# The 128-row block of the wide experts as three fp32r products, and the order of the first two experts

## The reference

```python
def moe_swiglu(h, router_w, w_gate, w_up, w_down):
    logits = xf @ router_w                      # 256 tokens, 8 experts
    top_val, top_idx = lax.top_k(logits, 2)
    gates = jax.nn.softmax(top_val, axis=-1)
    ...
    # for each expert, over the tokens that chose it (1024 -> 2816 -> 1024):
    y = (jax.nn.silu(x @ w_gate[e]) * (x @ w_up[e])) @ w_down[e]
    # out[token] += gate * y
```

## Time and profile before

| | |
|---|---|
| median of 3 runs | 1466.91 us (1465.32 to 1468.29) |
| the profiled execution, its own time | 1468.1 us |
| its span, first to last instruction | 1466.3 us |
| TensorE busy in the span | 96% |
| VectorE busy, ScalarE busy | 34%, 28% |
| bytes read from HBM | 383.77 MB |

### The profile page before, as it was taken

One profiled execution on the slowest core, in us unless ns is written; L12 is line 12 of the kernel. 1 busy time (PEld: TensorE's weight loads), 2 busy tenths in 40 slices (PEclk: granted clock), 3 DMA queues, 4 the chain that ended last, 5 costly groups with the idle time before them and its releaser, 6 DMA issues.

```text
span 1466.3 us, 23253 instructions
## 1 busy us (share of the span) xinstructions
PE 1414.9 (96%) x10140; PEld 1021.0 (70%) x10140; DVE 505.3 (34%) x747; ACT 407.2 (28%) x707; POOL 107.5 (7%) x133
## 2 busy tenths in 40 slices
PE   7999999999999999998999999999998999999996
PEld 7979988888888979988555645555544455555553
DVE  5667546666665657545100010101010100011112
ACT  5467436434345467444100000000000000000001
POOL 6200000000006000000100000101010100010100
PEclk9999999999999999998999999999999999999998
DMA  9308533555552217526746679999999996489995
GB/s 362 112 3 324 190 116 115 186 187 192 194 200 91 84 72 287 188 101 258 288 176 276 274 293 421 421 420 420 421 421 421 421 421 270 175 342 373 421 421 207
DMA packets 55138, 387.32 MB, mean 264 GB/s; under 512 B 6368, under 2 KB 6752, under 8 KB 9216
## 3 DMA queue, kind: packets, MB, share of 16 engines
q1 hardware_dynamic: 54112, 384.07, 66.1%
q10 hardware_dynamic: 432, 1.08, 0.2%
q0 software_dynamic: 496, 0.74, 0.2%
HBM read 383.77 MB, written 2.10 MB: 263 GB/s over the span
## 4 chain that ended last, share of the span: by engine, by line
PE 85%; DMA 6%; DVE 4%; ACT 3%; issue 1%; SPq 0%; DVEq 0%; ACTq 0%
PE banks L1845 40%; PE banks L1601 9%; PE banks L1603 9%; PE banks L1602 9%; PE banks L1774 6%; DMA raw_of_parts<-in_pieces_dram 4%; PE banks L1776 3%; DMA raw<-in_pieces_dram 2%; PE banks L1824 2%; PE banks L1809 2%; PE banks L1895 1%; PE banks L1721 1%; PE banks L1749 1%; PE banks L1625 1%; ACT w_high L827 1%
## 5 line engine op out<-in xcount | busy, mean ns | idle before, releaser
L1180 DVE TENSOR_TENSOR w_low<-raw,w_high 128x2048 fp32r<-128x2048 f32 x93 | 214.8, 2311 | 134.0 <-ACT w_high L827 133.9
L827 ACT ACTIVATE w_high<-raw 128x2048 fp32r<-128x2048 f32 x93 | 178.0, 1915 | 68.5 <-PE banks L1776 65.5
L1845 PE MATMUL banks<-raw,token_rows 128*64 128x256 f32 (+3 forms) x1480 | 161.3, 352 | 3.1 <-DMA raw<-in_pieces_dram 3.0
L1845 PE MATMUL banks<-raw_of_parts,token_rows 128*32 128x128 f32 (+4 forms) x1448 | 154.7, 344 | 2.8 <-DMA raw_of_parts<-in_pieces_dram 2.8
L1845 PEld LDWEIGHTS banks<-raw,token_rows 128*64 128x64 f32 (+2 forms) x1480 | 93.8, 132 | 71.6 <-issue 48.0
L1601 PE MATMUL banks<-rows,w_high 128*128 128x256 f32 x480 | 137.4, 286 | 2.0 <-DVE rows L1181 2.0
L1845 PEld LDWEIGHTS banks<-raw_of_parts,token_rows 128*64 128x64 f32 (+2 forms) x1448 | 94.5, 132 | 63.2 <-issue 42.5
L1601 PE MATMUL banks<-w_high,rows 128*128 128x256 f32 x480 | 137.4, 286 | 0.0
L1602 PE MATMUL banks<-rows,w_high 128*128 128x256 f32 x480 | 136.6, 285 | 0.0
L1603 PE MATMUL banks<-rows,w_low 128*128 128x256 f32 x480 | 136.6, 285 | 0.0
L1603 PE MATMUL banks<-w_high,rows 128*128 128x256 f32 x480 | 135.8, 283 | 0.0
(11 more groups left out here) (220 smaller groups left out, 1836.7 us busy)
## 6 DMA issues: line engine op xcount, KB each, us to landing
raw<-in_pieces_dram SPq DMA_DIRECT2D x183, 1024.0 KB, 7.2
raw_of_parts<-in_pieces_dram SPq DMA_DIRECT2D x90, 1024.0 KB, 17.8
raw_more<-in_pieces_dram SPq DMA_DIRECT2D x56, 1024.0 KB, 17.6
raw_of_mixed<-in_pieces_dram SPq DMA_DIRECT2D x28, 1024.0 KB, 19.2
phase<-in_mem_dram SPq DMA_DIRECT2D x2, 1024.0 KB, 6.7
early<-in_constants_dram SPq DMA_DIRECT2D x1, 1088.0 KB, 14.4
h_res<-in_x_dram SPq DMA_DIRECT2D x2, 512.0 KB, 4.2
phase<-in_mix_norm_post_dram SPq DMA_DIRECT2D x2, 512.0 KB, 4.4
```

Of the source, the lines that this page charges most:

```text
L827: return act.activation(out_, in_, ACT.Copy, scale=scale)
L1180: return dve.tensor_tensor(out_, in_, plain(high), ALU.subtract)
L1845: return pe.matmul(dst, stay, move, start=start, stop=stop, skip_group_check=True)
```

## The change

Each wide expert's block of 128 rows is computed with `product` in place of `plain_product`; its rest of 32 rows stays plain fp32. For that the parts of the weights are made in halves of a piece (128 x 1024). ACT copies a half into one of four buffers of high halves (`piece_high`, `make_high`), and DVE writes the low half over the piece itself in its slot (`make_low`), once the rest has used the piece (`rest_done`). A buffer of a high half is free again when TensorE has used the half two pieces before (`half_done`, `mixed`). The token rows are split once for each wide expert (`rows_high`, `rows_low`), and the transposed hidden rows in each step (`take_turned` on ACT and on DVE, `turned_parts`).

TensorE's order in a wide step becomes: the rest's gate and up columns, the rest's outputs of step s-1, gate, turns, up, gather, outputs. The hidden rows of the rest are turned by themselves (`turn_rest`).

The four buffers take memory, so the ring has 10 added slots in place of 12 (16 in all). `keep_h()` moves ahead of the first added slot, and SP no longer waits in it for the write to land; ACT waits for that (`h_kept`) before its first expert.

`EXPERT_AT` puts expert 1 ahead of expert 0, so the order of classes is narrow, wide, narrow, narrow, narrow, wide, narrow, narrow in place of wide, four narrow, wide, two narrow. The host lays the pieces out accordingly. The waits `gate_whole` and `up_whole` go.

```diff
+EXPERT_AT = (1, 0, 2, 3, 4, 5, 6, 7)
...
-OF_MIXED = 2
-MORE = 4
-ADDED = 2 * SPLIT + OF_MIXED + MORE
+ADDED = 2 * SPLIT + 4
...
+HALVES = 4
+HALF_PIECE = PIECE // 2
...
-STRAIGHT = {0: 3, 5: 3}
+STRAIGHT = {EXPERT_AT.index(0): 3, EXPERT_AT.index(5): 3}
...
-        raw_of_parts = sb("raw_of_parts", [P, 2 * SPLIT, PIECE])
-        token_rows = sb("token_rows", [P, 2, KT, SEQ])
-        raw_of_mixed = sb("raw_of_mixed", [P, OF_MIXED, PIECE])
+        with ExitStack() as as_low:
+            added_low = as_low.enter_context(nc.sbuf_tensor("added_low", [P, ADDED, PIECE], F32R))
+        added = sb("added", [P, ADDED, PIECE])
+        with ExitStack() as as_parts:
+            turned_parts = as_parts.enter_context(nc.sbuf_tensor("turned_parts", [P, 2, GROUPS, P], F32R))
...
-        raw_more = sb("raw_more", [P, MORE, PIECE])
+        with ExitStack() as as_low:
+            rows_low = as_low.enter_context(nc.sbuf_tensor("rows_low", [P, 2, KT, SEQ], F32R))
+        token_rows = sb("token_rows", [P, 2, KT, SEQ])
+        rows_high = sb("rows_high", [P, KT, P], F32R)
+        piece_high = sb("piece_high", [P, HALVES, HALF_PIECE], F32R)
...
-                sp.wait_ge(rank_full, 1)
-                sp.wait_ge(xn_ready, TT * 3 * DEPTH)
-                sp.wait_ge(h_kept, TT * 16)
 
             def load(c, r=0, n=None):
 
                 if c == more_from:
+                    keep_h()
                     sp.wait_ge(tile_full, after(DEPTH - 1, "xo"))
-                if c == more_from + ADDED - MORE:
-                    keep_h()
...
+                def take_rest(s):
+                    act.wait_ge(rest_done, MIXER * e + piece_of(piece(e, "up", s, of_step(s) - 1)) + 1)
+                    used = slice(0, QUARTER * blocks_per_step(s))
+                    act.activation(inner_rest[s % 2][used, :], banks[used, 6, 0:P], ACT.Silu).then_inc(rest_silu, 1)
+
+                def make_high(c, half):
+                    if piece_of(c) >= 2:
+                        if half:
+                            wait_mixed(act, c - 2)
+                        else:
+                            act.wait_ge(half_done, c - 2 - c_moe + 1)
+                    if half == 0:
+                        wait_loaded(act, c)
+                    move(high_half(c, half), raw_half(c, half)).then_inc(half_high, 1)
+
+                def take_turned(s):
+                    act.wait_ge(hidden_turned, step_at(e, s) + 1)
+                    move(turned_parts[:, 0, 0:blocks_per_step(s), :], turned_of(s)).then_inc(turned_high, 1)
+
+                def split_expert():
+                    if e == 0:
+                        act.wait_ge(x_by_dve, len(FIRST_BY_DVE))
+                        act.wait_ge(x_ready, len(FIRST_BY_ACT))
+                    else:
+                        act.wait_ge(x_ready, ROW_PAIRS * (e + 1))
+                    move(rows_high[:, :, :], token_rows[:, e % 2, :, 0:P]).then_inc(rows_high_ready, 1)
+                    for c, half in halves(e, "gate", 0):
+                        make_high(c, half)
+                    for s in range(WIDE_STEPS):
+                        ups = halves(e, "up", s)
+                        downs = halves(e, "down", s - 1) if s else []
+                        take_rest(s)
+                        for c, half in ups[:-1]:
+                            make_high(c, half)
+                        take_silu(s)
+                        if s:
+                            take_turned(s - 1)
+                        make_high(*ups[-1])
+                        for c, half in downs[:-1]:
+                            make_high(c, half)
+                        next_rows(s)
+                        if s:
+                            make_high(*downs[-1])
+                        if s + 1 < WIDE_STEPS:
+                            for c, half in halves(e, "gate", s + 1):
+                                make_high(c, half)
+                    for c, half in halves(e, "down", WIDE_STEPS - 1):
+                        make_high(c, half)
+                    take_turned(WIDE_STEPS - 1)
+                    take_output()
...
+                    act.wait_ge(h_kept, TT * 16)
...
+                def multiply_rest(s):
+                    dve.wait_ge(rest_silu, WIDE_STEPS * e + s + 1)
+                    used = slice(0, QUARTER * blocks_per_step(s))
+                    rest = inner_rest[s % 2][used, :]
+                    dve.tensor_tensor(rest, rest, banks[used, 6, P:2 * P], ALU.mult).then_inc(rest_hidden, 1)
+
+                def take_rest(s):
+                    dve.wait_ge(rest_turned, WIDE_STEPS * e + s + 1)
+                    used = slice(0, QUARTER * blocks_per_step(s))
+                    move(turned_rest[:, used], banks[:, 6, 2 * P:3 * P][:, used]).then_inc(rest_ready, 1)
+
+                def make_low(c, half):
+                    dve.wait_ge(half_high, half_number(c, half) + 1)
+                    if half == 0:
+                        dve.wait_ge(rest_done, c - c_moe + 1)
+                    low(low_half(c, half), raw_half(c, half), high_half(c, half)).then_inc(half_low, 1)
+
+                def split_expert():
+                    dve.wait_ge(rows_high_ready, e + 1)
+                    low(rows_low[:, e % 2, :, 0:P], token_rows[:, e % 2, :, 0:P], rows_high[:, :, :]).then_inc(rows_low_ready, 1)
+                    for c, half in halves(e, "gate", 0):
+                        make_low(c, half)
+                    for s in range(WIDE_STEPS):
+                        ups = halves(e, "up", s)
+                        downs = halves(e, "down", s - 1) if s else []
+                        multiply_rest(s)
+                        for c, half in ups[:-1]:
+                            make_low(c, half)
+                        if s:
+                            take_turned(s - 1)
+                        else:
+                            add_shares((0, 1))
+                        take_rest(s)
+                        make_low(*ups[-1])
+                        for c, half in downs[:-1]:
+                            make_low(c, half)
+                        multiply(s)
+                        if s:
+                            make_low(*downs[-1])
+                        else:
+                            add_shares((2, 3))
+                        if s + 1 < WIDE_STEPS:
+                            for c, half in halves(e, "gate", s + 1):
+                                make_low(c, half)
+                    for c, half in halves(e, "down", WIDE_STEPS - 1):
+                        make_low(c, half)
+                    take_turned(WIDE_STEPS - 1)
+                    take_output()
...
+                def split_columns(which, s):
+                    kind, dst = ("gate", "up")[which], banks[:, 4 + which, 0:width(s)]
+                    per = KT // of_step(s) // 2
+                    at = 0
+                    for c, half in halves(e, kind, s):
+                        pe.wait_ge(half_low, half_number(c, half) + 1)
+                        w_h, w_l = (view(t, 0, per, width(s)) for t in (high_half(c, half), low_half(c, half)))
+                        for k in range(per):
+                            ins = product(dst, (rows_high[:, at, :], rows_low[:, e % 2, at, 0:P]), (w_h[:, k, :], w_l[:, k, :]),
+                                          at == 0, at == KT - 1)
+                            at += 1
+                        count_half(ins, half)
+
+                def split_outputs(s, of=None):
+                    pe.wait_ge(hT_ready, step_at(e, s) + 1)
+                    if e and s == 0:
+                        pe.wait_ge(sum_added, 4 * e)
+                    for i in range(of_step(s)) if of is None else of:
+                        c = piece(e, "down", s, i)
+                        for j in range(FPS):
+                            pe.wait_ge(half_low, half_number(c, j) + 1)
+                            w_h, w_l = high_half(c, j), low_half(c, j)
+                            for hh in range(2):
+                                half = slice(hh * HALF, (hh + 1) * HALF)
+                                ins = product(banks[:, hh, :], [turned_parts[:, n, 2 * i + j, :] for n in range(2)],
+                                              (w_h[:, half], w_l[:, half]), s == 0 and i == 0 and j == 0, True)
+                            count_half(ins, j)
...
+                def split_expert():
+                    for s in range(WIDE_STEPS):
+                        if s == 3:
+                            ahead = pe.mark_branch_hint_location()
+                        last = s == WIDE_STEPS - 1
+                        if s:
+                            pe.wait_ge(rest_ready, WIDE_STEPS * e + s)
+                        rest_columns(0, s)
+                        rest_columns(1, s)
+                        if s:
+                            rest_outputs(s - 1)
+                        else:
+                            pe.wait_ge(rows_low_ready, e + 1)
```

(26 more changed lines are left out.)

225 lines of the change are left out of this document (122 added, 103 removed).

## The result

The changed kernel takes 1424.47 us (median of 4 runs, 1423.46 to 1433.8; in the last one the mean granted clock was 0.943, against about 0.99). The kernel before took 1466.33 beside it. The ratio is 0.9727, 95% interval 0.9685 to 0.9769. Five runs on another chip gave 1422.18 (1421.79 to 1423.87) against 1466.66, ratio 0.9701 [0.9687, 0.9714]. Predicted was 1424.

A forecast was written before the change was run, and what follows sets the result against it. TensorE, busy 96% of the span, was taken as the bound. Two wide experts gain 40.0 us and waiting for pieces falls by 3.1, so 1466.9 - 43.1 gives 1424 us; forecast band 1416 to 1432 (0.56), range 1409 to 1445.

The forecast's parts named there:

- Products: Wide experts: fp32r matmuls at 0.2296 us, three replacing two fp32 records of 0.429, save 22.1 us per wide expert.
- faster pace: Rival, wide experts' products: fp32r costs no more array time than an fp32 record, 0.2145; 11 us more gained, 1413; chance 0.13.
- ScalarE and VectorE: Full wide step: ACT needs 14.5 us and DVE 16.6, both below TensorE's 23.6, so no stall, about 1 us spare.
- handoffs rival: Full wide steps: semaphore handoffs to a fourth half end each step 2 us late, ten steps 20 us, 1444; chance 0.16.
- slower case: Rival, `make_low`: low parts on DVE bound a wide step from 2.1 us a half; about 1475 to 1507; chance 0.05.
- Stalls at the ends: Wide expert: TensorE stalls 0.7 us at the start and 1.4 in the last step, leaving a gain of 20.0 us.
- Order and ring: Expert order and two slots fewer: waits for pieces total 13.7 us against 16.8 before, 3.1 less.
- wide start: Wide expert behind the third narrow one begins with an empty ring: 5.7 us, less 0.7 of start stall covered, 5.0 waiting.
- The sign: Expert phase: TensorE's waits for DMA should be about 14 us, most of it behind the run's third narrow expert.
- Sum: Whole kernel: 40.0 us from two wide experts plus 3.1 less waiting, 43.1 off the median 1466.9, giving 1424.
- the term for waiting: Expert phase: waits of 7.7, 5.0, 0.5 and 0.5 us, 13.7 in all against 16.8, so 3.1 less.
- DMA rival: Narrow runs and wide start: wide experts do not fill the ring, 15 us more waiting, 1439; chance 0.08.

The follow-up runs named there:

- low twice: Changed kernel with a second VectorE operation on each half, the low half copied onto itself before TensorE may use it: 1461.63 us, ratio 0.9964.
- The reordered last step: Changed kernel, two narrow experts before the first wide one, both up halves of a wide expert's last step made before silu and hidden rows: 1415.57 us, ratio 0.9656.
- the fill: The reordered last step plus ten transposes into an unused bank behind each of the first three pieces of the first wide expert: 1415.44 us, ratio 0.9657.
- two products: Changed kernel without the product of low token part by high weight part, and the same for outputs, in the wide experts' block: 1381.53 us, ratio 0.9418.

## Why the prediction was right

**Products.** Forecast 0.2296 each and 22.1 us a wide expert. Output products stood 0.227 apart, a step took 23.5 (23.6 forecast), a wide expert saves 20.5 with its two stalls (20.0). The faster pace is refuted: products in the experts run like those of the earlier trace rows. The prediction gives that rival's 0.2145 as the distance of the fp32 records; in the earlier trace rows they stand 0.429 apart, and 0.2145 is half of that. The figure of the Trainium skill (TensorE: Matmul & The Clock Gate, Part 1) lies 5 to 6% below what either trace shows.

**ScalarE and VectorE.** Forecast 14.5 and 16.6 us a step, measured 13.2 to 14.3 and 16.0 to 16.7; halves 1.06 and 1.22 against 1.03 and 1.22. There was no stall in a full step. The handoffs rival is refuted for this kernel, and the experiments show how near it was: with 1.86 a half a step takes 26.9, with two buffers 29.25, and TensorE waits 27 and 45 us for VectorE. The slower case would have needed 2.1 by the prediction; low twice puts the point just above 1.86 (the estimate above), so it was nearer than forecast.

**Stalls at the ends.** Forecast 0.7 and 1.4; measured 1.1 at the first start, hidden at the second, 0.42 where the ring is full, and 1.4 twice. The reordered last step takes the 1.4 away and shows its cause. At the first start ScalarE stands for 0.49 us, with nothing in the profile that it waits for, before it splits the token rows (at 763.95); at the start with 0.42 it does not. That is most of the difference, and what ScalarE does in it is not known.

**Order and ring.** Waiting for pieces, forecast: 7.7 at the third narrow expert, 5.0 at the wide start behind it, 0.5 at the first wide expert, 0.5 at the last: 13.7. Measured in the first profile: 7.4 (77.1 - 69.7), 7.9 (141.3 - 133.4), none at the first wide expert, whose 0.5 over 133.4 is the longer wait for VectorE, and none at the last (64.0 as before). In all 15.3; the saving is 1.5 and not 3.1. In the second profile: 6.6 (76.3 - 69.7) and 6.1 (139.5 - 133.4), in all 12.7; the saving is 4.1. The wide start is too low in both, by 2.9 and 1.1; the third narrow expert is too high, by 0.3 and 1.1, as it had to be if two slots cost less than 5.0. At the first wide expert the prediction read its own change wrongly: it left `keep_h` at 681.75, where the kernel before issues it behind eight loads that begin at 677.63 us, but the change moves it ahead of them. It issued at 677.55 and the loads followed from 678.39 on, 4.2 us earlier than reckoned, or 1.8 when the earlier start of the experts is taken off. The sign that the view of waits would show about 14 us for pieces did not come true (9.5).

**The wide start** is the place where a mechanism was missed. Its timeline in the kernel after, and two-microsecond windows beside it:

```profile
1121.12 1.94 PE L1987 MATMUL banks<-raw,turned 128*64 128x512 f32 x8 [0.55 <-DMA raw<-in_pieces_dram]
1123.61 1.08 PE L1987 MATMUL banks<-raw,token_rows 128*32 128x128 f32 x32 [0.55 <-DMA raw<-in_pieces_dram]
1126.00 1.08 PE L1987 MATMUL banks<-added,token_rows 128*32 128x128 f32 x32 [1.31 <-DMA added<-in_pieces_dram]
1128.49 1.94 PE L1987 MATMUL banks<-added,token_rows 128*32 128x128 f32 x32 [1.40 <-DMA added<-in_pieces_dram]
1130.96 1.93 PE L1987 MATMUL banks<-added,token_rows 128*32 128x128 f32 x32 [0.54 <-DMA added<-in_pieces_dram]
1132.83 0.80 PE L1743 MATMUL banks<-piece_high,rows_high 128*128 128x512 f32 x1
```

```profile
1126.00:1128.00 2.00, 1.08 (x32) 0.81 (x32) 2.00 (x3) 2.00 (x3) 0.00 (x0) 1.00 1.04 434
1128.00:1130.00 2.00, 1.51 (x31) 1.39 (x32) 2.00 (x3) 0.62 (x1) 0.00 (x0) 0.55 1.02 418
1130.00:1132.00 2.00, 1.46 (x28) 0.98 (x24) 0.63 (x1) 0.00 (x0) 0.00 (x0) 0.50 1.00 410
1132.00:1134.00 2.00, 2.00 (x23) 1.39 (x15) 0.29 (x1) 0.28 (x1) 0.00 (x0) 0.50 1.03 430
1134.00:1136.00 2.00, 2.00 (x8) 1.60 (x7) 0.00 (x0) 0.49 (x1) 0.00 (x0) 0.75 0.97 406
```

The pieces land 2.4 to 2.5 apart and the DMA moves 410 to 434 GB/s, as forecast. Between them TensorE has 1.1 us of work, and after two gaps of 1.3 and 1.4 its granted clock falls to 0.50 (from 2.4 to 1.2 GHz). The fourth piece's columns then take 1.93 in place of 1.08 (0.85), and the first six steps of the gate products take 2.48 in place of 1.46 (1.02, against the start at 1131.98 of the kernel with two narrow experts first). That is 1.9 us. The second profile of the same kernel is the control: its clock did not fall there, and the same four rows read

```profile
1123.96 1.08 PE L1987 MATMUL banks<-raw,token_rows 128*32 128x128 f32 x32 [0.55 <-DMA raw<-in_pieces_dram]
1126.36 1.08 PE L1987 MATMUL banks<-added,token_rows 128*32 128x128 f32 x32 [1.32 <-DMA added<-in_pieces_dram]
1128.85 1.08 PE L1987 MATMUL banks<-added,token_rows 128*32 128x128 f32 x32 [1.41 <-DMA added<-in_pieces_dram]
1131.32 1.08 PE L1987 MATMUL banks<-added,token_rows 128*32 128x128 f32 x32 [1.39 <-DMA added<-in_pieces_dram]
```

with an interval of 139.5 in place of 141.3: 1.8 less. Without the clock the start thus costs 6.0 to 6.1 where 5.0 was forecast. Of the rest, 0.3 is the start stall that it covers, 0.42 there and not 0.7; the remaining 0.7 was not taken apart. Nine profiles here have a wide expert of the changed scheme that starts on an empty ring, the one with the fill left out; the granted clock fell in six of them (not in the second profile, in two products and in low twice), so what the start costs is partly chance.

**Sum.** 2 x 20.5, less the 0.5 of the first wide expert, and 1.5 of waiting make 42.0; the first profile has 42.4 from first product to last scatter. With the 4.1 of the second it is 44.6, and that profile has 45.1. The forecast, 43.1, lies between them, as it does between the differences of the medians, 41.9 on the first chip and 44.5 on the second. So the mechanism holds and the products' term is right to 0.5, but that the median came within 0.5 us of 1424 is luck: the term for waiting was 1.6 too good in one execution and 1.0 too bad in the other, and the 2.4 us ahead of the experts are in the first profile and in neither term. The DMA rival (1439, 15 us of waiting more) is refuted: the wide experts fill the ring, and the run behind each begins at 78.1 and 69.7.

## What to carry to other kernels

When the parts of a weight are made beside the products, set a step out in order, with every wait on a buffer, before you trust the busy sums: VectorE at 71% of a step cost nothing here, while the same work with half the buffers made the kernel slower than without the change. Making the long stages faster moves the stalls to where the ring is empty, so look at the order of stages together with it: in the kernel before, the order was worth 14.9 us and two slots 3.3; in the changed kernel, a better order was worth 6.0 and two slots 9.4 (by the medians, the last two across chips). Expect that a term right to half a microsecond in a steady step is off by one to three at a start with an empty queue: here the wait itself was 1.1 longer than forecast, and in some executions the clock fell as well (1.8). And read more than one profile of a kernel before you explain two microseconds.

## What the runs showed of the hardware

- The granted clock fell to 0.50 (1.2 GHz) behind two gaps of 1.3 and 1.4 us, between stretches of 1.1 us of work. It happened in one execution of the changed kernel and not in another with the same gaps (1.32, 1.41, 1.39), and what decides it these runs do not show. Ten transposes in each gap held it at 1.00 in the one profile that has them.
- In fp32r a 512-column matmul started every 0.227 to 0.233 us in the stretches read here (0.2296 in the earlier trace rows, 0.227 from 801.05, 0.233 from 1135.31 to 1136.94 in the changed kernel). A plain fp32 record of the same shape took 0.429, two of them a product; half a record is 0.2145, 12 to 19 ns less than an fp32r matmul, which was not explained.
- Two slots of the ring (5.0 us of DMA time) cost 3.5 to 4.3 us at the end of a run, in four comparisons (72.4 to 76.1; 77.1 or 76.3 to 80.6; 64.0 to 67.6). Why it is less was not tried.
